# Norm, turns, up and down products of the last MLP as one stage, with the norm scaled and turned by halves of the columns

## The reference, cut to what matters

```python
h = rms_norm_2(x, mlp_norm_g[l])                       # x: 256 x 1024
x = x + jnp.square(jax.nn.relu(h @ w_up[l])) @ w_down[l]   # w_up 1024 x 4096, w_down 4096 x 1024
...
return rms_norm_2(x, final_norm_g)
```

## Time and profile before

| | us |
|---|---|
| median of 3 runs | 2220.16 |
| the three runs | 2218.01, 2220.16, 2228.01 |
| the profiled execution | 2217.21 |
| its span (first to last instruction) | 2215.5 |
| mean granted TensorE clock of the span | 0.885 |

### The profile page before, as it was taken

How to read it: one execution, slowest core, us unless ns; L and a number is a source line. 1 busy time by engine, 2 the same in 40 slices (tenths; PEclk the granted TensorE clock), 3 DMA queues, 4 the chain that set the end, 5 groups by cost and what they waited for, 6 DMA issues and landing times.

```text
span 2215.5 us, 20631 instructions
## 1 busy us (share of the span) xinstructions
PE 1690.3 (76%) x6478; PEld 1022.0 (46%) x6478; DVE 1483.4 (67%) x3052; ACT 799.6 (36%) x2068; POOL 645.6 (29%) x524
## 2 busy tenths in 40 slices
PE   7697877757767765886787487665767889988988
PEld 3473333622323444332344432554333455668976
DVE  3357776698656678965666896658776454565634
ACT  1212353224324421432452135213554343444532
POOL 0002434344433443543343354425453000000000
PEclk9698988879898887989889789887889999999999
DMA  8268999999999999999999999999999765564442
GB/s 295 101 231 342 412 406 395 421 400 422 419 417 414 408 421 408 402 419 420 403 377 422 385 391 420 421 421 421 380 402 395 285 230 200 217 240 149 173 169 96
DMA packets 108828, 761.54 MB, mean 344 GB/s; under 512 B 13104, under 2 KB 14000, under 8 KB 18608
## 3 DMA queue, kind: packets, MB, share of 16 engines
q0 software_dynamic: 73728, 536.90, 59.1%
q1 hardware_dynamic: 32544, 215.45, 25.3%
q10 hardware_dynamic: 2448, 7.87, 0.9%
HBM read 759.12 MB, written 1.05 MB: 343 GB/s over the span
## 4 chain that ended last, share of the span: by engine, by line
PE 39%; DMA 23%; DVE 21%; ACT 10%; issue 5%; DVEq 1%; POOL 1%; PEldq 0%; ACTq 0%; SPq 0%; PEld 0%; POOLq 0%
DMA sb_work<-in_peer_uv,sb_expert 19%; PE ps_acc L1358 12%; PE bank L444 5%; DVE sb_work L1322 4%; PE bank L1171 4%; DVE sb_x L1330 4%; DMA sb_wring<-in_peer_w_q 2%; PE bank L1844 2%; PE bank L511 2%; PE bank L697 2%; PE bank L512 2%; PE bank L513 2%; PE ps_acc L511 2%; PE ps_acc L513 2%; PE ps_acc L512 2%
## 5 line engine op out<-in xcount | busy, mean ns | idle before, releaser
L2342 POOL DMA_INDIRECT sb_work<-in_peer_uv,sb_expert x512 | 641.5, 1253 | 1060.3 <-PE ps_acc L1358 476.1
L1358 PE MATMUL ps_acc<-sb_work,sb_diag 128*128 128x512 f32 x1304 | 697.7, 682 | 326.8 <-ACT sb_diag L1347 275.6
L1322 DVE CUSTOM_DVE_ANT_0 sb_work<-sb_work,sb_h 128x1024 f32<-128x1024 f32 x512 | 619.9, 1223 | 214.0 <-DMA sb_work<-in_peer_uv,sb_expert 201.9
L1358 PEld LDWEIGHTS ps_acc<-sb_work,sb_diag 128*128 128x128 f32 x1304 | 266.5, 217 | 699.8 <-issue 690.8
L1338 ACT ACTIVATE sb_dots<-sb_dots 128x1 f32<-128x1 f32 x512 | 102.2, 200 | 527.8 <-DVE sb_dots L1322 482.3
L1330 DVE SCALAR_TENSOR_TENSOR sb_x<-sb_work,sb_weight,sb_x 128x1024 f32<-128x1024 f32 x186 | 238.4, 1282 | 80.5 <-ACT sb_weight L1339 80.5
L505 DVE TENSOR_TENSOR sb_work_r<-sb_wring,sb_work_r 128x2048 fp32r<-128x2048 f32 (+1 forms) x76 | 138.1, 1840 | 126.7 <-ACT sb_work_r L498 126.7
L444 PE MATMUL bank<-sb_wring,sb_hT 128*128 128x512 f32 (+2 forms) x392 | 157.6, 561 | 26.1 <-DVEq L283 19.4
L498 ACT CAST sb_work_r<-sb_wring 128x2048 fp32r<-128x2048 f32 (+1 forms) x76 | 115.2, 1545 | 123.6 <-PE ps_acc L513 43.9
L1339 ACT ACTIVATE sb_weight<-sb_dots,sb_share 128x1 f32<-128x1 f32 x512 | 150.7, 294 | 16.7
L1171 PE MATMUL bank<-sb_hT,sb_wring 128*128 128x128 f32 x1024 | 127.3, 290 | 22.3 <-DMA sb_wring<-in_peer_w_q 20.2
(11 more groups left out here) (316 smaller groups left out, 2079.2 us busy)
## 6 DMA issues: line engine op xcount, KB each, us to landing
sb_wring<-in_w_mix SPq DMA_DIRECT2D x36, 1024.0 KB, 8.7
sb_wring<-in_peer_w_q SPq DMA_DIRECT2D x32, 1024.0 KB, 12.1
sb_wring<-in_w_gate SPq DMA_DIRECT2D x32, 1024.0 KB, 4.8
sb_wring<-in_hyb_w_in SPq DMA_DIRECT2D x20, 1024.0 KB, 5.0
sb_wring<-in_w_up SPq DMA_DIRECT2D x16, 1024.0 KB, 4.9
sb_wring<-in_w_down SPq DMA_DIRECT2D x16, 1024.0 KB, 4.8
sb_wring<-in_mla_w_uq SPq DMA_DIRECT2D x12, 768.0 KB, 10.0
sb_wring<-in_hyb_w_out SPq DMA_DIRECT2D x8, 1024.0 KB, 5.8
```

What stands on the lines that cost most here:

```text
L1322: e.tensor_tensor_reduce(u, u, h[:, t, :], 1.0, 0.0, ALU.mult, ALU.add, dots[:, i:i + 1]).then_inc(dot_ready, 1)
L1358: last = e.matmul(ps_acc[:, b * 512:(b + 1) * 512], diag[:, number % DIAGS, :], ring[:, n % RING, D + b * 512:D + (b + 1) * 512], start=k ...
L2342: pool.indirect_dma_start(ring[:, n % RING, :], None, a["peer_uv"], bass.IndirectOffsetOnAxis(ap=expert[:, t, n % P:n % P + 1], axis=0)).t ...
```

## The change

The three stages of the MLP become one, without barriers between them. `norm_both` with a pair returns its parts instead of making a stage, and `project_split` does too; the up stage calls the norm's parts first and the down parts last. Within the norm, the scalings are cut into halves of 512 columns in the order (tile 0, half 0), (tile 1, half 0), (tile 0, half 1), (tile 1, half 1). VectorE subtracts the first two turned units before it scales the last two halves. Each weight block of up block 0 waits only for its own two turned units. The first two splits of down are taken out of `project_split`'s order (`ahead` = 2) and issued in the loop over the up blocks, as the splits of a ninth block. In the last round ScalarE issues the second of them before the four roundings. TensorE waits in the first half of down for each hidden block by a new signal, `hidden_made`.

```diff
@@ project_split
-        def project_split(pair, w, chunks, cols, empty, engine, ring):
+        def project_split(pair, w, chunks, cols, empty, engine, ring, ahead, ready):
...
                     for i, m in enumerate(ms):
+                        if c0 == 0:
+                            e.wait_ge(*ready(i))
                         split_wait(e, m)
...
-                    for what, i in order:
+                    for what, i in order[ahead:]:
...
-            stage(pe=pe, act=other("act"), dve=other("dve"))
+            return pe, other("act"), other("dve"), [i for _, i in order[:ahead]]
@@ norm_both
-            turned_pe, turned_act, turned_dve, _ = (
-                turn_split_parts(H, pair, [(0, 0), (0, 1), (1, 0), (1, 1)]) if pair else (None,) * 4)
+
+            order = [(0, 0), (1, 0), (0, 1), (1, 1)]
+            turned_pe, turned_act, turned_dve, units = turn_split_parts(H, pair, order) if pair else (None,) * 4
+            row_made = [made] + [first_row.plan() for _ in range(2)] + [number] if pair else [made, number]
+            row_sem = [first_row.sem] * (len(row_made) - 1) + [gain_used.sem]
 
             def pe(e):
-                e.wait_ge(first_row.sem, made)
-                turned_pe(e, 0)
-                turned_pe(e, 1)
-                e.wait_ge(gain_used.sem, number)
-                turned_pe(e, 2)
-                turned_pe(e, 3)
+                for i in range(4):
+                    e.wait_ge(row_sem[i], row_made[i])
+                    turned_pe(e, i)
...
-                if pair:
-                    for i in range(4):
+                if pair is None:
+                    for t in range(2):
+                        e.scalar_tensor_tensor(dst(t), X(t), stat[:, 8 + t:9 + t], gain[:, :], ALU.mult, ALU.mult
+                                               ).then_inc(row_sem[t], 1)
+                    return
+                for i, (t, q) in enumerate(order):
+                    cols = slice(512 * q, 512 * q + 512)
+                    e.scalar_tensor_tensor(dst(t)[:, cols], X(t)[:, cols], stat[:, 8 + t:9 + t], gain[:, cols],
+                                           ALU.mult, ALU.mult).then_inc(row_sem[i], 1)
+                    if i % 2:
+                        turned_dve(e, i - 1)
                         turned_dve(e, i)
...
@@ the up and down parts
+        down_pe, down_act, down_dve, first_down = project_split(
+            hidden, a["w_down_2"], 32, D, add_residual, "dve", (0, 1), 2, lambda i: (hidden_made.sem, hidden_at[i]))
+        next_splits = [ms for ms, _, _, _ in up_plan[1:]] + [first_down]
 
         def up_pe(e):
+            norm_pe(e)
             for b, (ms, units, _, _) in enumerate(up_plan):
                 for i, m in enumerate(ms):
+                    for u in mlp_units[2 * i:2 * i + 2] if b == 0 else ():
+                        u.wait_emptied(e)
                     split_wait(e, m)
...
+            down_pe(e)
+
         def up_act(e):
+            norm_act(e)
             for b, (_, units, sq_v, _) in enumerate(up_plan):
-                if b + 1 < len(up_plan):
-                    split_act(e, up_plan[b + 1][0][0])
+                split_act(e, next_splits[b][0])
                 for j, u in enumerate(units):
                     u.wait_full(e)
                     e.activation(units_2[:, (4 * b + j) % 8, :], u.ap[:, 0:SEQ], ACT.Relu).then_inc(u.free, 1)
+                if b + 1 == len(up_plan):
+                    split_act(e, next_splits[b][1])
                 for j in range(4):
                     e.wait_ge(squared.sem, sq_v[j])
                     e.copy(hidden[0][b][:, j, :], units_2[:, (4 * b + j) % 8, :]).then_inc(turned_hi.sem, 1)
                 if b + 1 < len(up_plan):
-                    split_act(e, up_plan[b + 1][0][1])
+                    split_act(e, next_splits[b][1])
+            down_act(e)
```

More of the change, by code:

```diff
@@ L2213, in dve @@
                 e.wait_ge(gain_landed.sem, g_value)
-                for t, done_sem in ((0, first_row.sem), (1, gain_used.sem)):
-                    e.scalar_tensor_tensor(dst(t), X(t), stat[:, 8 + t:9 + t], gain[:, :], ALU.mult, ALU.mult
-                                           ).then_inc(done_sem, 1)
-                if pair:
-                    for i in range(4):
+                if pair is None:
[9 more added lines that the diff above has]
+                        turned_dve(e, i - 1)
                         turned_dve(e, i)
-            stage(pe=pe if pair else None, act=act, dve=dve)
-            return (first_row.sem, made), (gain_used.sem, number)
+            if pair is None:
+                stage(act=act, dve=dve)
+                return (first_row.sem, made), (gain_used.sem, number)
+            return pe, act, dve, units
         hidden = T_quads, quads(tok_r[:, 0:32 * SEQ])
@@ L2226, in build @@
         mlp_pair = quads(hT_r[:, :]), quads(low)
-        norm_both(H, a["mlp_norm_g_2"], mlp_pair)
+        norm_pe, norm_act, norm_dve, mlp_units = norm_both(H, a["mlp_norm_g_2"], mlp_pair)
         up_plan = []
@@ L2237, in build @@
         units_2 = h[:, :, :].rearrange("p a b -> p (a b)").rearrange("p (n s) -> p n s", s=SEQ)
+        hidden_made = Signal(sem("hidden_made"))
+        hidden_at = [hidden_made.plan() for _ in up_plan]
+        down_pe, down_act, down_dve, first_down = project_split(
+            hidden, a["w_down_2"], 32, D, add_residual, "dve", (0, 1), 2, lambda i: (hidden_made.sem, hidden_at[i]))
+        next_splits = [ms for ms, _, _, _ in up_plan[1:]] + [first_down]
         def up_pe(e):
+            norm_pe(e)
             for b, (ms, units, _, _) in enumerate(up_plan):
                 for i, m in enumerate(ms):
+                    for u in mlp_units[2 * i:2 * i + 2] if b == 0 else ():
+                        u.wait_emptied(e)
                     split_wait(e, m)
@@ L2265, in up_act @@
                 if b + 1 < len(up_plan):
-                    split_act(e, up_plan[b + 1][0][1])
+                    split_act(e, next_splits[b][1])
+            down_act(e)
         def up_dve(e):
+            norm_dve(e)
             for b, (_, units, _, hi_v) in enumerate(up_plan):
-                if b + 1 < len(up_plan):
-                    split_dve(e, up_plan[b + 1][0][0])
+                split_dve(e, next_splits[b][0])
                 for j, u in enumerate(units):
@@ L2275, in up_dve @@
                     e.tensor_tensor(v, v, v, ALU.mult).then_inc(squared.sem, 1)
-                if b + 1 < len(up_plan):
-                    split_dve(e, up_plan[b + 1][0][1])
+                split_dve(e, next_splits[b][1])
                 for j in range(4):
                     e.wait_ge(turned_hi.sem, hi_v[j])
-                    e.tensor_tensor(hidden[1][b][:, j, :], units_2[:, (4 * b + j) % 8, :], hidden[0][b][:, j, :],
-                                    ALU.subtract)
+                    last = e.tensor_tensor(hidden[1][b][:, j, :], units_2[:, (4 * b + j) % 8, :], hidden[0][b][:, j, :],
+                                           ALU.subtract)
+                last.then_inc(hidden_made.sem, 1)
+            down_dve(e)
         stage(pe=up_pe, act=up_act, dve=up_dve)
-        project_split(hidden, a["w_down_2"], 32, D, add_residual, "dve", (0, 1))
         rows_made = norm_both(H, a["final_norm_g_2"])
```

## The result

The changed kernel takes 2209.99 us (median of 7 runs, 2204.75 to 2214.61) against 2220.38 us for the kernel before in runs beside it (7 runs). The ratio is 0.9947 with a 95% interval of 0.9931 to 0.9963. It is faster, by 0.53%. A ratio of 1 lies outside the interval, and the size is about at the bound of 0.5% that the prediction used for a change that can be told from none. The forecast was 2210.5 us and 0.44%. The profiled execution took 2204.75 us around a span of 2203.0, 12.5 us shorter than the span before.

What follows compares the result with a forecast made beforehand. TensorE was taken to bound the up and down stretches, a ScalarE and VectorE chain the border between. 6.95 + 2.3 + 0.4 = 9.7 us off the median 2220.16 gave 2210.5 us, range 2205.5 to 2216.5.

Steps and rivals of the forecast that it cites:

- Step 1: Border of up and down: first down product follows the last up product after 0.12 us; 6.95 us saved.
- The cover: TensorE's first down block hides the second down split, with 0.74 us of slack left.
- Step 2: Start of down: no products at the lower clock; 2.91 us saved in this execution, 2.3 us for a median.
- Step 3: Norm and turns: half scalings of 0.70 us bring the first up product 0.4 us earlier.
- Step 4: Hidden-block waits, extra increments and w_down loads cost nothing; a w_down block lands 4.8 us after its issue.
- The slower rival: Down stretch: split chain exceeds its 0.95 us slack, paid 14 times; 2232 us at 2.5 longer; chance 0.04.
- The sum: Whole edit: 9.7 us gained for a median, 10.3 us against the profiled execution; chance 0.66.
- The chance of 0.28: Whole kernel: chance given to being faster by over 0.5%.
- 0.09: Chance of the clock giving more at both borders: gain 11.6 us, time 2208.6 us.
- a quarter of 0.66: Share of the likeliest case, chance 0.66 and gain 9.7 us, counted as faster by over 0.5%.

Runs made afterwards that it cites:

- filled idle time: Kernel before plus 36 filler products of 256 columns at the head of the down stage, while the first down split is made; 2222.80 us (one run).
- down alone: Against the kernel before, only up and down products share a stage, two down splits ahead; the norm keeps its own stage; 2209.49 us, ratio 0.9951.
- filled norm: Changed kernel plus 27 filler products of 256 columns ahead of the first turn in the norm; 2207.87 us (one run).

## Why the prediction held, step by step

*Step 1, the idle time:* 6.95 us forecast, 7.07 - 0.12 = 6.95 us measured. The border is 0.12 or 0.13 us in all nine profiles in which down is merged. The cover (the second split beside the first down block) had 0.77 us left for 0.74 forecast, and putting that split behind other work showed the cover's edge, after 0.62 us.

*Step 2, the slow products:* 2.91 us against this execution, 2.94 measured. The wider claim, that a median would get 2.3 us with ends of 1.4 and 2.9, can't be tested one by one, but both ends were seen (1.53 and 2.94). The cause is shown by the filled idle time. The section of the Trainium skill that the prediction names (TensorE: Matmul & The Clock Gate, Part 1, "What's actually happening"), by which the number of slow matmuls varies from run to run, agrees with these runs: 7 and 14 behind the same border, 13 and 28 behind the same norm.

*Step 3, the norm:* 0.4 us forecast, 0.93 measured, of which 0.27 went to a longer low stretch in this pair. This is the mis-sized term. Two things were wrong in it. The prediction let the first up product wait for the whole length of the row of eight matmuls of the third and fourth unit, 1.94 us (0.97 a unit), but a row's length overlaps the next instruction. In the changed kernel the first up product starts 1.62 us after that row's start (2010.33 - 2008.71), so 0.32 us were too much. The other 0.20 us are the third unit's start, 5.00 us after the first scaling for 5.20 forecast. The prediction put it 0.26 us behind the end of its scaling, as for the first unit, and it came 0.05 us behind it (2008.71 against 2007.91 + 0.75). The half scaling was put too low (0.70 for 0.747), with no harm, since two of them take 1.41 us in a row.

*Step 4, what costs nothing:* w_down still lands 4.8 us after its issue, and TensorE is never idle in the down stretch. The slower rival needed 14 late splits; there was none. The last part grew by 0.14 us, which no step foresaw. It is 9.67 to 9.74 us in the kernels in which either border is kept and 9.83 to 9.89 in those in which both are gone. The timelines show where: ScalarE's sum of squares for the final norm starts 1.25 or 1.26 us after the last down product in the first kind (2207.03 in the kernel before) and 1.54 or 1.55 us in the second (2194.68 in the changed one), in all thirteen profiles. Why ScalarE leaves the last stage border that much later stays open.

*The sum:* 10.3 us against this execution and 10.4 measured in the pieces. Part of that agreement is luck: the norm gave 0.53 us more than forecast, and the longer low stretch at the start of up (0.27) and the last part (0.14) took most of it back. The time, 2210.5 for 2209.99, is nearer than the scatter allows one to claim. The chance of 0.28 for more than 0.5% was low for what came out (0.53%, 0.61% and, with down alone, 0.49%), and its two parts, 0.09 and a quarter of 0.66, make only 0.26. The sum was right and the bound lies inside the scatter, so that the two cases were nearer to even.

## What to carry to other kernels

At a barrier, ask which work behind it needs nothing that the barrier guards. Here it was a weight split whose input had landed long ago; issuing it ahead of the barrier's place was worth 7 us at one border, and the slow products behind the idle time another 1.5 to 3. Once engines run without a barrier, the order inside each of them decides: a split moved ahead of four roundings, and scalings ahead of subtractions, gave 4.3 us more with no work removed (2.2 for the stops, 1.45 for the norm, and 0.6 for a shorter low stretch, whose cause isn't shown). When a kernel scatters by as much as an edit can give, divide its profiles at fixed events and compare the pieces.

## What the runs showed of the hardware

- Two idle times of one length had different effects. After 2.65 us the granted clock fell, and only 0.8 us after the products had resumed (2111.68 against 2110.86; 0.93 in the window between, 0.51 behind it). After 2.68 us (2120.04 - 2117.36) no product was slow. A shorter one behind eight turns was enough in the filled norm: the clock fell within the 2.0 us of the pause (0.87 over it, 0.50 behind it).
- The low stretch behind the same norm was 2.9 us in one profile and 6.1 in two others. The 3.2 us between them were worth 1.4 us of the span.
- A merged row of TensorE is longer than the time for which it holds up the next instruction: 1.97 us against 1.62 for eight turns.
